# Gated blocks of the plain FFNs made with features on partitions, and the relative bias begun two steps later

## The reference

```
def swiglu(u, w_gate, w_up, w_down):
    return (jax.nn.silu(u @ w_gate) * (u @ w_up)) @ w_down
```

## Time and profile before

| | |
|---|---|
| median of 3 runs | 2260.1 us (2250.1 to 2260.55) |
| span of the profiled execution | 2252.3 us |
| time of the profiled execution by the same clock as the runs | not recorded beside the span |
| TensorE busy with matmuls | 2129.6 us (95%) |
| DVE, ACT, GpSimd busy | 61%, 44%, 11% |
| granted TensorE clock, mean | 0.979 of full speed |
| HBM | 406.45 MB read, 182 GB/s over the span |

### The profile page before, as it was taken

How to read it: one execution, slowest core, us unless ns; L and a number is a source line. 1 busy time by engine, 2 the same in 40 slices (tenths; PEclk the granted TensorE clock), 3 DMA queues, 4 the chain that set the end, 5 groups by cost and what they waited for, 6 DMA issues and landing times.

```text
span 2252.3 us, 30439 instructions
## 1 busy us (share of the span) xinstructions
PE 2129.6 (95%) x12378; PEld 1748.3 (78%) x12378; DVE 1383.1 (61%) x1999; ACT 999.4 (44%) x1569; POOL 252.7 (11%) x290
## 2 busy tenths in 40 slices
PE   7999888999999999978989989999999999998999
PEld 5777777767777777767767877777899887777997
DVE  4544877757456545675745566657676465666673
ACT  3443453425444444345434435434555345444552
POOL 0000200112000200021300021420000112400000
PEclk9999999999999999989999999999999998999999
DMA  9877763437767785752746654335566562444664
GB/s 323 264 253 240 193 179 93 160 102 250 253 227 231 249 259 198 224 198 94 244 159 199 203 137 124 94 114 166 163 187 194 153 163 75 125 158 138 187 189 139
DMA packets 374524, 411.08 MB, mean 183 GB/s; under 512 B 27527, under 2 KB 319723, under 8 KB 374384
## 3 DMA queue, kind: packets, MB, share of 16 engines
q1 hardware_dynamic: 367536, 388.37, 55.6%
q0 software_dynamic: 6848, 20.76, 3.1%
HBM read 406.45 MB, written 2.62 MB: 182 GB/s over the span
## 4 chain that ended last, share of the span: by engine, by line
PE 79%; DVE 9%; ACT 5%; DMA 2%; issue 2%; POOL 2%; SPq 0%; DVEq 0%; POOLq 0%; ACTq 0%
PE ps L171 76%; PE ps L174 3%; DVE arena L180 3%; ACT whi L177 2%; DVE wlo L180 2%; ACT arena L177 1%; DVE arena L192 1%; DVE tmp L180 1%; DVE small L198 1%; ACT uh L177 1%; DMA x<-in_x 1%; DVE tmp L192 1%; POOL x L180 0%; DMA tmp<-in_rel_bias 0%; ACT L177 0%
## 5 line engine op out<-in xcount | busy, mean ns | idle before, releaser
L180 DVE TENSOR_TENSOR wlo<-raw,whi 128x1024 fp32r<-128x1024 f32 (+1 forms) x592 | 726.0, 1246 | 414.3 <-ACT whi L177 411.6
L177 ACT ACTIVATE whi<-raw 128x1024 fp32r<-128x1024 f32 (+1 forms) x592 | 608.4, 1050 | 321.3 <-DMA raw<-in_w_up 81.2
L171 PE MATMUL ps<-whi,uh 128*128 128x512 f32 (+1 forms) x1282 | 528.0, 412 | 14.1 <-DVE ul L180 4.4
L171 PE MATMUL ps<-wlo,uh 128*128 128x512 f32 (+1 forms) x1282 | 507.9, 397 | 0.0
L171 PE MATMUL ps<-whi,ul 128*128 128x512 f32 (+1 forms) x1282 | 411.1, 396 | 0.0
L171 PE MATMUL ps<-whi,arena_r 128*128 128x512 f32 x1184 | 371.9, 392 | 3.5 <-DVE arena_r L180 2.5
L171 PEld LDWEIGHTS ps<-whi,uh 128*128 128x128 f32 x1282 | 244.5, 191 | 96.3 <-issue 31.4
L171 PE MATMUL ps<-uh,whi 128*128 128x256 f32 (+1 forms) x992 | 284.8, 287 | 10.2 <-DVE arena L192 7.2
L171 PEld LDWEIGHTS ps<-whi,ul 128*128 128x128 f32 x1282 | 243.2, 191 | 58.2 <-DVE ul L180 0.5
L171 PEld LDWEIGHTS ps<-wlo,uh 128*128 128x128 f32 x1282 | 245.0, 191 | 51.0
L171 PE MATMUL ps<-ul,whi 128*128 128x256 f32 (+1 forms) x992 | 280.5, 283 | 0.0
(11 more groups left out here) (219 smaller groups left out, 1809.0 us busy)
## 6 DMA issues: line engine op xcount, KB each, us to landing
arena<-in_mod_w SPq DMA_DIRECT2D x62, 1024.0 KB, 6.8
raw<-in_w_in SPq DMA_DIRECT2D x90, 512.0 KB, 3.7
raw<-in_ffn_w_gate SPq DMA_DIRECT2D x176, 256.0 KB, 4.0
raw<-in_ffn_w_up SPq DMA_DIRECT2D x176, 256.0 KB, 4.7
raw<-in_ffn_w_down SPq DMA_DIRECT2D x88, 512.0 KB, 3.6
raw<-in_w_up SPq DMA_DIRECT2D x88, 512.0 KB, 3.9
raw<-in_w_down SPq DMA_DIRECT2D x44, 512.0 KB, 3.5
raw<-in_hyb_w_in SPq DMA_DIRECT2D x32, 512.0 KB, 4.9
```

The source lines that it names most:

```text
L171: return Nothing() if self.raw is None else self.raw.matmul(out, l, r, start=start, stop=stop)
L177: return Nothing() if self.raw is None else self.raw.activation(out, src, func, **kw)
L180: return Nothing() if self.raw is None else self.raw.tensor_tensor(out, a, b, op)
```

## The change

From block `by_token` on (block 6 in n = 0, block 4 in n = 2, 3 and 5) a block is made by a new function, `pe_feat_block`: weights are stationary (128 x 128), all 256 tokens of `uT` are moving, and a block (c, i) now stands for one tile of 128 features of column block c, with the gate in one half of the bank and the up product in the other. It takes 48 matmuls of N = 256 where `pe_block` took 24 of N = 512, and the result has features on partitions, as `hT` wants it. PE's transposes for these blocks go. ACT's high part and DVE's low part read `sg` in SBUF in place of the turned copy in PSUM; ACT waits for `h` where it waited for `h_tr`, and the silu of block j waits for `h_lo` of block j - 2 where it waited for the transposes of that block. `turns_lead` keeps the high and low parts ahead of the silu where the silu needs them. `block_of` tells the down part which block its row k comes from. In the block with i = 1, `used` of the four units is signalled behind matmuls 30, 36, 42 and 48 of 48.

Both generators of the relative bias begin with two empty steps, so that the product for head h stands ahead of block 2h + 7 and its spreading copy at the beginning of step 2h + 6.

```diff
--- before.py
+++ after.py
@@ -948,6 +948,7 @@
             self.mods = (4, 6, 8, 10, 12, 14, 16, 18)
             self.bank = [(4, 5, 0, 1)[j % 4] for j in range(last)]
             self.turn_bank = [2 if j == 2 else 6 for j in range(last)]
+            self.by_token = 4
         else:
             self.first = o = 2 * OPEN
             self.order = [(c, t) for c in range(NC) for t in range(T)]
@@ -957,7 +958,17 @@
             self.loads = [0] * o + [0, 4] * (NC - OPEN)
             self.mods = (8, 10, 12, 14, 15, 17, 18, 20)
             self.bank = [4, 5, 0, 1, 2, 3] + [(4, 5, 0, 1)[j % 4] for j in range(last - o)]
-            self.turn_bank = [6 if j % 2 == 0 or j > 9 else 7 if j < 4 else 2 for j in range(last)]
+            self.turn_bank = [6 if j % 2 == 0 else 7 if j < 4 else 2 for j in range(last)]
+            self.by_token = o
+
+    def turns_lead(self, j):
+
+        return len(self.silu[j]) != 1 or any(i >= self.by_token and i + 2 in self.silu[j] for i in self.turns[j])
+
+    def block_of(self, k, t):
+
+        j = self.order.index((k // 2, k % 2))
+        return j if j >= self.by_token else self.order.index((k // 2, t))
 
 
 COURSES = [Course(0), Course(1)]
@@ -989,16 +1000,34 @@
             gate, up = ffn_up(M, n, c)
             units[c] = pe_units(pe, M, KD, 512, "a", (gate, 0, 256), (up, 256, 512))
             M.uid["up", n, c] = units[c][-1][0]
-        last = pe_block(pe, M, fill(pe, M, C.bank[j], ("h", n, j)), units[c], n - 1, t)
+        bank = fill(pe, M, C.bank[j], ("h", n, j))
+        if j < C.by_token:
+            last = pe_block(pe, M, bank, units[c], n - 1, t)
+        else:
+            last = pe_feat_block(pe, M, bank, units[c], t)
         if t == 0:
             last.then_inc(*pe.ev("up0", n, c))
         for i in C.turns[j]:
-            pe_ffn_turn(pe, M, n, i)
+            if i < C.by_token:
+                pe_ffn_turn(pe, M, n, i)
         if j > 1:
             pe_mod_sum(pe, M, 3)
         if j in C.mods:
             pe_mod(pe, M, 7)
     pe.drain()
+
+
+def pe_feat_block(pe, M, bank, units, i):
+
+    rows = [(uid, v[:, r, :], r == v.hi.shape[1] - 1) for uid, v in units for r in range(v.hi.shape[1])]
+    for part in range(2):
+        at = part * 256 + i * P
+        for k, (uid, v, ends) in enumerate(rows):
+            pe.wait_ge(*pe.on("lo", uid))
+            last = mm3(pe, bank[:, part * S:part * S + S], v[:, at:at + P], M.uT[:, k, :], k == 0, k == KD - 1)
+            if i and part and ends:
+                last.then_inc(*pe.ev("used", uid))
+    return last
 
 
 def pe_ffn_turn(pe, M, n, j):
@@ -1013,15 +1042,13 @@
 
 def pe_ffn_out(pe, M, n):
     l, i = n // 3, n % 3 // 2
-    pe_final(pe, M, ("s", n), ffn_views(M)[0], lambda k, t: [pe.on("h_lo", n, course(n).order.index((k // 2, t)))], NF,
+    pe_final(pe, M, ("s", n), ffn_views(M)[0], lambda k, t: [pe.on("h_lo", n, course(n).block_of(k, t))], NF,
              M.A["ffn_w_down"][l, i].rearrange("(k p) n -> p k n", p=P), lambda t: [("ln_v", "y", n, t)], LATE, 0,
              lambda k: pe_ffn_beside(pe, M, n, k))
 
 
 def pe_ffn_beside(pe, M, n, k):
 
-    if k == 0:
-        pe_ffn_turn(pe, M, n, 2 * NC - 1)
     if k in MOD_ROWS:
         pe_mod_sum(pe, M, 5)
         pe_mod(pe, M, 7)
@@ -1030,13 +1057,16 @@
 def turned_h(M, n, j):
     C = course(n)
     c, t = C.order[j]
+    if j >= C.by_token:
+        hT, sg = ffn_views(M)
+        return hT[:, 2 * c + t, :], sg[j % 2]
     return (ffn_views(M)[0][:, 2 * c:2 * c + 2, t * P:(t + 1) * P],
             M.bank(C.turn_bank[j])[:, 0:256].rearrange("p (a b) -> p a b", a=2))
 
 
 def act_ffn_hi(act, M, n, j):
     dst, src = turned_h(M, n, j)
-    act.wait_ge(*act.on("h_tr", n, j))
+    act.wait_ge(*(act.on("h_tr", n, j) if j < course(n).by_token else act.on("h", n, j)))
     act.activation(dst.hi, src, ACT.Copy).then_inc(*act.ev("h_hi", n, j))
 
 
@@ -1052,7 +1082,7 @@
     _, sg = ffn_views(M)
     act.wait_ge(*(act.on("used", M.uid["up", n, c]) if t else act.on("up0", n, c)))
     if j > 1:
-        act.wait_ge(*act.on("h_tr", n, j - 2))
+        act.wait_ge(*act.on("h_tr" if j - 2 < C.by_token else "h_lo", n, j - 2))
     act.activation(sg[j % 2], M.bank(C.bank[j])[:, 0:S], ACT.Silu).then_inc(*act.ev("silu", n, j))
 
 
@@ -1070,7 +1100,7 @@
             act.tick()
         turns = [lambda i=i: act_ffn_hi(act, M, n, i) for i in C.turns[j]]
         silu = [lambda i=i: act_ffn_silu(act, M, n, i) for i in C.silu[j]]
-        for f in silu + turns if len(silu) == 1 else turns + silu:
+        for f in turns + silu if C.turns_lead(j) else silu + turns:
             f()
         if j in C.mods:
             act_mod(act, M, 7)
@@ -1090,7 +1120,7 @@
             dve.tick()
         turns = [lambda i=i: dve_ffn_lo(dve, M, n, i) for i in C.turns[j]]
         hs = [lambda i=i: dve_ffn_h(dve, M, n, i) for i in C.silu[j]]
-        for f in hs + turns if len(hs) == 1 else turns + hs:
+        for f in turns + hs if C.turns_lead(j) else hs + turns:
             f()
         if j > 1:
             dve_mod_fix(dve, M, 3)
@@ -2832,6 +2862,7 @@
 
 def pe_rel(pe, M):
     v = rel_views(M)
+    yield from blank(2)
     for h in range(8):
         yield
         bank = fill(pe, M, 2, ("rel_row", h))
```

## The result

The changed kernel takes 2269.9 us (median of 16 runs, 2256.1 to 2275.4) against 2259.6 us before (16 runs, 2250.1 to 2266.8). The ratio is 1.0045, interval 1.0032 to 1.0058: slower by 0.45%, some 10.3 us. The forecast was 14.4 us faster.

A forecast was written before the change was run, and what follows sets the result against it. The prediction took PE's own work to bound the kernel, busy with matmuls for 95% of the span. -14.7 + 2.8 - 8.4 + 5.9 = -14.4 us, put on the median 2260.1: 2245.7 us, range 2232 to 2258.

The forecast's parts named there:

- Transposes and cadence: 70 blocks in n = 0, 2, 3, 5: transposes gone, -14.7 us; matmuls at 0.1174 us each, +2.8 us.
- rival F: New blocks: weight loads set the pace at 188 ns each, 3.4 us more a block, some 2480 us; chance 0.01.
- Start of the bias: Start of n = 5: the wait for the table and the slow block behind it go, 8.4 us off.
- The later end of the bias is hidden: End of n = 5's up part: last product ahead of block 21, covered by a down part of some 50 us.
- Rival C: n = 5 gives back its gain: bias-product waits at upper bound or over, or table late; 2254 us, chance 0.14.
- What is late next: n = 5: copies queue behind later units, PE waits 1.1 us at five bias products; 5.9 us, bounds 2 and 10.
- In n = 0, 2 and 3 this is free: Later `used` and units wanted earlier cost nothing there; 4.4 us of cover left, a cost only behind 4 us of delay.
- Rival E: Later `used` of two units starves all 35 column blocks; 2288 us at 1.2 us each; chance 0.07.
- rival D: Less PE work in the FFNs is met by longer waits for transfers between stages; 2256 to 2262 us, chance 0.08.

The follow-up runs named there:

- e5_feat_not5: The changed kernel with new blocks in n = 0, 2 and 3 only, n = 5 and the bias as before the change: 2253.9 us, ratio 0.9971.
- e1_bias_early: The changed kernel with the two empty steps taken out, so the bias begins as before: 2260.4 us, ratio 1.0012.
- e3_bias_bank6: The changed kernel with the bias products in PSUM bank 6 in place of bank 2: 2258.9 us, ratio 1.0006.
- e10_rows_outer_bank6: The changed kernel with weight rows outermost in n = 2, 3 and 5, bias in bank 6, last block in bank 7: 2245.0 us, ratio 0.9936.
- e2_bias_late_only: The kernel before with the two empty steps in both bias generators and nothing else: 2259.1 us, ratio 1.0008.
- e8_late_used_only: The kernel before with the first two `used` of late column blocks signalled 1.2 us later, nothing else: 2267.3 us, ratio 1.0035.
- e4_bias_one: The changed kernel with one empty step for the bias in place of two: 2245.5 us, ratio 0.9943.
- e6_rows_outer: The changed kernel with weight rows outermost, gate and up in two banks, in n = 2, 3 and 5: 2253.8 us, ratio 0.9968.
- e7_rows_outer_one: The changed kernel with weight rows outermost in n = 2, 3 and 5 and one empty step for the bias: 2243.2 us, ratio 0.9926.
- e9_one_from_six: The changed kernel with one empty step and feature blocks only from block 6 on in n = 2, 3 and 5: 2247.3 us, ratio 0.9943.

## Why the prediction was wrong, point by point

**Transposes and cadence: right.** Two blocks and what stands between them in n = 2 take 12.89 us after (553.11 to 566.00) and 13.26 before (545.73 to 558.99), 0.185 us a block; the forecast was 0.17, and e5_feat_not5 gives 0.17 (0.11 to 0.23). The sustained cadence is 0.117 us, so rival F is out.

**Start of the bias: right in size.** The stretch is 9.4 us shorter, 8.4 without the product that left it. Not all of this is the doing of the move: in e1_bias_early, with the new blocks and the early bias, the same stretch was 3.5 us shorter already.

**"The later end of the bias is hidden": wrong.** This is the step that failed outright. I looked for who needs the last head's result, and found nobody for 50 us. But the product also holds a bank, and the down part needs banks 0 to 3 at once. The price is 7.5 us of idle time and 3.2 in a down part that begins at the lower clock; e3_bias_bank6 and e10_rows_outer_bank6 take both away with the bank alone, and e2_bias_late_only makes a smaller copy of them in the old kernel. No rival had it. Rival C's condition, waits over their upper bound, did come true, but with it alone the forecast would have been -14.4 + 9.6 = -4.8 us, near C's -6.0 and still faster.

**"What is late next": the mechanism right, the size wrong.** The waits stand where the forecast put them and come from the late `used` (e8_late_used_only makes them; e4_bias_one and e6_rows_outer take them away, all but one in the latter). The term was 5.9 us with an upper bound of 10; it measured 15.5. The idle time itself, 7.8 us, lies within the bounds. What put the term outside is that the price of an idle stretch was counted as the stretch alone, while two of the six brought the lower clock, for 5.0 us. Two more things were missed: the product waits for the copy of the previous rows too, 0.5 us behind the spreading copy; and in the block looked at above the second unit's transfer took 0.9 us longer and not up to 0.4, though not in most of the others.

**"In n = 0, 2 and 3 this is free": nearly.** The first feature block in n = 2, 3 and 5 takes 1.1 us longer, 3.4 in all. The figures for the delay were in the prediction; the cover was read in a later column block, where two units are split at a time, and not in the first, for which DVE splits all four in step 2. Rival E did not come: no column block waits in n = 2 or 3 behind the first feature block.

**The sum as measured.** -11.9 (70 x 0.17) + 3.4 - 8.4 + 15.5 + 7.5 + 3.2 = +9.3 us, against +10.3 by the medians. For n = 5 alone the same terms give -3.1 + 1.1 - 8.4 + 15.5 + 7.5 + 3.2 = +15.8 us, against +15.7 in the traces.

**Still open.** In n = 1, whose own work the change doesn't touch, the profiled execution lost 8.3 us. From PE's transposes of 16 x 16 at the end of n = 0 to its transposes of 128 x 128 just ahead of the first block of n = 2 pass 216.0 us before and 224.4 after. In the two experiments that keep the old blocks it is 216.6 (e2_bias_late_only) and 221.1 us (e8_late_used_only), in the eight others with new blocks 219.3 to 224.5. All nine kernels with new blocks are thus longer here than two of the three without, but e8_late_used_only shows that 5 us can be lost without them, and there is one trace of each kernel. So it isn't settled whether this is chance or tied to the change. If it is tied, it is rival D: less work in the FFNs met by longer waits elsewhere. e5_feat_not5, which lost 3.3 us here in its trace, reached its forecast all the same. The loss may be what e4_bias_one and e7_rows_outer_one lack of their sums (-16.9 against 13 measured, -20.3 against 16.7), and why e9_one_from_six didn't gain; that is argued only. The sum lies just outside the interval of e4_bias_one (9.3 to 16.5 us) and within that of e7_rows_outer_one (11.8 to 21.5).

## What to carry to other kernels

When work is moved later, ask not only who reads its result but what it holds until then: a PSUM bank, a buffer, a semaphore that a later stage waits for. When a loop's order changes, list the times at which it gives buffers back, and follow the later ones through transfer and conversion to everything that is queued behind them, the second of two copies too. Where a move goes by steps, try one step more and one less: here one step in place of two put the copies behind units that had landed, and that decided the sign.

## What the runs showed of the hardware

The granted clock fell behind idle stretches of PE of 1.66 and 2.10 us in the changed kernel, 1.78 in e1_bias_early, 1.66, 1.76 and 1.82 in e3_bias_bank6, and 1.44 and 1.92 in e8_late_used_only. It did not fall behind those of 0.79 to 1.16 in the changed kernel, nor behind 1.69 and 1.76 in e1_bias_early and 1.71 in e8_late_used_only. So at these lengths the length of the wait doesn't tell. Where it fell behind one of these in the new blocks, 16 to 26 cadences of N = 256 ran at the lower level: a short wait had a price of its own length, or of its length and 1.5 to 2.5 us more. I had not expected that of waits this short.

At the lower level a matmul of N = 256 came every 0.213 us and one of N = 512 every 0.427; at the higher level it was 0.117 and 0.233. Half the clock costs 1.82 times the time, not twice. The Trainium skill ("TensorE: Matmul & The Clock Gate", Back-to-back issue gap) gives N / 1.2 ns for an isolated gap at the lower level, 213 and 427 ns, and the trace agrees; for the higher it gives N / 2.4 + 2.5, 109 and 216 ns, and the trace has 117 and 233 in these pairs of weight load and float32r product, so for them the measured figures decide.

The name that the profile puts behind an idle stretch was a low part, a copy and "issue" for one and the same wait for bank 2, in three kernels. It was the taking away of the bank that settled it.
